# Two reversed chunks: one stationary operand with the keys of two chunks per recurrence level, and another order at the end of the recurrence

## What is computed

```python
f = lb + (1.0 - lb) * jax.nn.sigmoid(f_pre)
log_f, k, q, v = jnp.log(f), 1.0 - f, jax.nn.silu(q_pre), i_in
def step(state, inp):
    qc, kc, vc, lfc = inp
    b = jnp.cumsum(lfc, axis=2)
    o_inter = jnp.einsum('bhtd,bhde->bhte', qc * jnp.exp(b), state)
    decay = jnp.where(causal, jnp.exp(b[t] - b[s]), 0.0)          # [t, s, d]
    a = jnp.einsum('bhtd,bhsd,bhtsd->bhts', qc, kc, decay)
    o_intra = jnp.einsum('bhts,bhse->bhte', a, vc)
    b_last = b[:, :, -1:, :]
    state = jnp.exp(b_last) * state + jnp.einsum('bhsd,bhse->bhde', kc * jnp.exp(b_last - b), vc)
    return state, o_inter + o_intra
o = o * lax.rsqrt(jnp.mean(o * o, axis=-1, keepdims=True) + NORM_EPS)
o = o.reshape(B, S, E) * out_norm * jax.nn.silu(g_pre)
return o @ w_out
```

## Time and profile before

| | |
|---|---|
| median of 3 runs | 2952.06 us (2950.47 to 2953.12) |
| profiled execution, its own time | 2953.08 us |
| its span | 2951.2 us |
| PE busy | 2922.4 us, 99% of the span |
| DVE, POOL, ACT busy | 80%, 44%, 40% |
| granted TensorE clock | 0.999 of 2.4 GHz |
| the recurrence | from 1555.7 to 1684 us of the span |

### The profile page before, as it was taken

How to read it: one execution, slowest core, us unless ns; L and a number is a source line. 1 busy time by engine, 2 the same in 40 slices (tenths; PEclk the granted TensorE clock), 3 DMA queues, 4 the chain that set the end, 5 groups by cost and what they waited for, 6 DMA issues and landing times.

```text
span 2951.2 us, 43795 instructions
## 1 busy us (share of the span) xinstructions
PE 2922.4 (99%) x16066; PEld 2617.8 (89%) x16066; DVE 2363.7 (80%) x4421; ACT 1192.1 (40%) x1853; POOL 1296.6 (44%) x747
## 2 busy tenths in 40 slices
PE   8999999999999999999999999999999999999999
PEld 7778999999998888888889988999999998888887
DVE  7538999989878888888356747999888878888887
ACT  6543334444433333333435533333444433333333
POOL 4133565334444444442447443654444444444441
PEclk9999999999999999999999999999999999999999
DMA  4032558999999999998321032659999999999995
GB/s 156 31 106 86 172 177 319 372 357 355 379 377 398 362 361 359 363 361 293 100 93 44 30 107 79 196 179 366 363 360 374 359 399 387 363 362 361 359 365 212
DMA packets 346148, 799.76 MB, mean 271 GB/s; under 512 B 27984, under 2 KB 192080, under 8 KB 345680
## 3 DMA queue, kind: packets, MB, share of 16 engines
q1 hardware_dynamic: 235200, 478.09, 46.3%
q0 software_dynamic: 73728, 268.47, 23.8%
q10 hardware_dynamic: 37008, 50.41, 4.6%
HBM read 694.10 MB, written 102.76 MB: 270 GB/s over the span
## 4 chain that ended last, share of the span: by engine, by line
PE 97%; DVE 1%; ACT 1%; issue 0%; DMA 0%; POOL 0%; DVEq 0%; SPq 0%
PE PS L1644 29%; PE PS L1646 29%; PE PS L1645 29%; PE PS L1865 3%; PE PS L1946 2%; PE PS L1844 1%; PE PS L1774 1%; PE PS L1775 1%; PE PS L1821 1%; DVE resid L1089 1%; ACT arena L690 0%; PE PS L1809 0%; PE PS L1654 0%; PE PS L1655 0%; PE PS L1949 0%
## 5 line engine op out<-in xcount | busy, mean ns | idle before, releaser
L677 ACT ACTIVATE w_hi<-w_raw 128x1024 fp32r<-128x1024 f32 x607 | 641.8, 1059 | 816.5 <-PE PS L1646 678.7
L1644 PE MATMUL PS<-x_hi,w_hi 128*128 128x384 f32 (+1 forms) x2564 | 897.2, 350 | 0.0
L1646 PE MATMUL PS<-x_hi,w_lo 128*128 128x384 f32 (+1 forms) x2564 | 886.4, 346 | 0.0
L1645 PE MATMUL PS<-x_lo,w_hi 128*128 128x384 f32 (+1 forms) x2564 | 884.9, 345 | 0.0
L1644 PE MATMUL PS<-w_hi,x_hi 128*128 128x512 f32 x1744 | 679.6, 390 | 0.8 <-ACT arena L771 0.8
L1646 PE MATMUL PS<-w_hi,x_lo 128*128 128x512 f32 x1744 | 678.6, 389 | 0.0
L1645 PE MATMUL PS<-w_lo,x_hi 128*128 128x512 f32 x1744 | 678.5, 389 | 0.0
L614 POOL DMA_INDIRECT arena<-in_v_t,arena x256 | 427.7, 1671 | 553.0 <-DVE resid L1387 525.1
L603 POOL TENSOR_TENSOR w_lo<-w_raw,w_hi 128x1024 fp32r<-128x1024 f32 x167 | 414.3, 2486 | 513.6 <-ACT w_hi L677 513.6
L1364 DVE TENSOR_TENSOR w_lo<-w_raw,w_hi 128x1024 fp32r<-128x1024 f32 x440 | 536.7, 1220 | 108.0 <-ACT w_hi L677 105.1
L614 POOL DMA_INDIRECT arena<-in_u_rows,arena x256 | 384.6, 1502 | 498.6 <-DVE arena L1371 444.3
(11 more groups left out here) (205 smaller groups left out, 2360.6 us busy)
## 6 DMA issues: line engine op xcount, KB each, us to landing
w_raw<-in_u_t SPq DMA_DIRECT2D x256, 512.0 KB
w_raw<-in_v_t SPq DMA_DIRECT2D x256, 512.0 KB
acts_dram<-arena ACTq DMA_DIRECT2D x256, 192.0 KB
gates_dram<-arena SPq DMA_DIRECT2D x24, 2048.0 KB
arena<-acts_dram SPq DMA_DIRECT2D x256, 192.0 KB
arena<-gates_dram SPq DMA_DIRECT2D x64, 768.0 KB
w_raw<-in_hg_t SPq DMA_DIRECT2D x40, 512.0 KB
w_raw<-in_pq_t SPq DMA_DIRECT2D x32, 512.0 KB
```

The source lines that it names most:

```text
L677: act.activation(w_hi[:, slot, :], w_raw[:, slot, :], ACT.Copy).then_inc(hi_ready, 1)
L1644: pe.matmul(ps, wh, xh, start=start, stop=False)
L1645: pe.matmul(ps, wh, xl, start=False, stop=False)
L1646: return pe.matmul(ps, wl, xh, start=False, stop=stop)
```

## The change

The tokens of chunks 2 and 3 are held in reverse (`TIME`), from the input on; the host puts the rows back at the end. In a reversed chunk the first half of a block's places holds the later tokens. So at each level the places of keys in chunks 0 and 1 are those of queries in chunks 2 and 3, and the other way round. The keys of chunk c and of chunk c + 2, 64 each, fill one stationary operand of 128 columns without gaps, and the moving operand holds the 64 queries of chunk c and the 64 of chunk c + 2. That is two matmuls of 128 x 128 for four of 128 x 64 at each of 56 levels. The masks drop the products between the two chunks.

What follows from it:

- `scale_level` is two instructions of 256 elements (keys, then queries) in place of one of 512.
- `take_diff` and the exponents read and write in patterns of two halves; their counts and element counts stay.
- `tensor_tensor_scan`, the cumulated sum, is two scans of 256 per head, the second one backward, in place of one of 512.
- The masks of the levels are 256 columns wide each; `mask_bits` grows from 1696 to 2592 columns of two bytes. `causal` gets a reversed twin for the attention in chunks 2 and 3.
- The gain of the output norm moves from DVE's `gate_head` (now a `tensor_tensor`) to ACT's copy in `head_out`.
- At the end of the recurrence spread 4 comes ahead of values and output of head 7, hss and the spreads 5 to 7 come earlier, and `project` of half rows 0 and 1 is split in two and laid between spreads. ACT's `gated_high(4)` comes ahead of `head_out(7)`, DVE's `gated_low(4)` and `gated(5)` ahead of `gate_head(7)`.

```diff
@@ -84,7 +84,10 @@
-M_LEVEL, M_IOTA, M_PAIR, M_COLS = SEQ, SEQ + 8 * P, SEQ + 9 * P, SEQ + 9 * P + 2 * TOPK
+M_SAME, M_LEVEL = SEQ, SEQ + P
+M_IOTA = M_LEVEL + LEVELS * SEQ // 2
+M_PAIR, M_COLS = M_IOTA + P, M_IOTA + P + 2 * TOPK
+TIME = [*range(SEQ // 2), *range(SEQ - P - 1, SEQ // 2 - 1, -1), *range(SEQ - 1, SEQ - P - 1, -1)]
@@ -218,19 +221,21 @@
                 yield "gate", part // KC, part % KC
                 part += 1
         if n >= 2 and (n - 2) % 8 == 7:
+            if n > 8 * HEADS:
+                yield "spread", 4, 0
             yield "values", (n - 2) // 8, 0
             yield "ho", (n - 2) // 8, 0
         if n % 8 == 0 and n >= 16:
             yield "hss", n // 8 - 2, 0
             if n == 8 * HEADS:
                 yield "project", 0, (2, 3)
-    yield "project", 0, (0, 1)
-    yield "spread", 4, 0
+    yield "spread", 5, 0
     yield "hss", HEADS - 1, 0
-    yield "spread", 5, 0
+    yield "project", 0, (0,)
     yield "spread", 6, 0
+    yield "project", 0, (1,)
+    yield "spread", 7, 0
     yield "project", 2, (0, 1, 2, 3)
-    yield "spread", 7, 0
 def plan():
...
@@ -408,11 +412,21 @@
-        def keys_and_queries(h, m):
-            both = arena[:, h * SEQ:h * SEQ + SEQ]
-            return bass.AP(both.tensor, both.offset,
-                           [list(both.ap[0]), [2 * m, SEQ // (2 * m)], [HEADS * SEQ + m, 2], [1, m]])
+        def of_halves(ap, first, second, step, count, inner, size):
+            return bass.AP(ap.tensor, ap.offset + first,
+                           [list(ap.ap[0]), [second - first, 2], [step, count], [inner, size]])
+        def level_keys(ap, m):
+            return of_halves(ap, 0, SEQ // 2 + m, 2 * m, P // m, 1, m)
+        def level_queries(ap, m):
+            return of_halves(ap, m, SEQ // 2, 2 * m, P // m, 1, m)
+        def backward(ap):
+            n = ap.shape[-1]
+            return bass.AP(ap.tensor, ap.offset + n - 1, [list(ap.ap[0]), [-1, n]])
@@ -632,16 +646,16 @@
+                half, b = SEQ // 2, gb[:, h, :]
-                    b4 = chunked(gb[:, h, :])
-                    ins = pool.tensor_tensor(chunked(d), b4[:, :, P - 1:P].broadcast_to([P, TT, P]), b4,
-                                             ALU.subtract)
+                    ins = pool.tensor_tensor(of_halves(d, 0, half, P, 2, 1, P),
+                                             of_halves(b, P - 1, half, P, 2, 0, P),
+                                             of_halves(b, 0, half, P, 2, 1, P), ALU.subtract)
-                    bb = gb[:, h, :].rearrange("p (b m) -> p b m", m=2 * m)
-                    ins = pool.tensor_tensor(d.rearrange("p (b m) -> p b m", m=2 * m), bb,
-                                             bb[:, :, m - 1:m].broadcast_to([P, SEQ // (2 * m), 2 * m]),
-                                             ALU.subtract)
+                    ins = pool.tensor_tensor(of_halves(d, 0, half, 2 * m, P // m, 1, 2 * m),
+                                             of_halves(b, 0, half, 2 * m, P // m, 1, 2 * m),
+                                             of_halves(b, m - 1, half + m, 2 * m, P // m, 0, 2 * m), ALU.subtract)
@@ -948,17 +962,16 @@
-                def halves(ap):
-                    return ap.rearrange("p (b s m) -> p b s m", s=2, m=P >> k)
-                act.activation(halves(scaling(n))[:, :, 0], halves(d)[:, :, 0], ACT.Exp, scale=-1.0)
-                act.activation(halves(scaling(n))[:, :, 1], halves(d)[:, :, 1], ACT.Exp)\
-                   .then_inc(sem("level_exp"), 1)
+                m = P >> k
+                by_part = scaling(n).rearrange("p (w s b m) -> p w s b m", w=2, s=2, m=m)
+                act.activation(by_part[:, 0], level_keys(d, m), ACT.Exp, scale=-1.0)
+                act.activation(by_part[:, 1], level_queries(d, m), ACT.Exp).then_inc(sem("level_exp"), 1)
-                free(act.activation(gq[:, h, :], PSb(("ho", h)), ACT.Copy), ("ho", h))
+                g = G_AT["out"] + h
+                free(act.activation(gq[:, h, :], PSb(("ho", h)), ACT.Copy, scale=gain[:, g:g + 1]), ("ho", h))
@@ -1007,8 +1020,8 @@
             gated_high(3)
             roots(1)
             next_high(BASE["hg_g"] + HEADS - 1)
+            gated_high(4)
             head_out(HEADS - 1)
-            gated_high(4)
             roots(2)
             gated_high(5)
             gated_high(6)
...
@@ -1448,8 +1461,11 @@
-                dve.tensor_tensor_scan(gb[:, h, :], keep, diff[:, h % 2, :], 0.0, ALU.mult, ALU.add)\
-                   .then_inc(sem("cumulated"), 1)
+                early, late = slice(0, SEQ // 2), slice(SEQ // 2, SEQ)
+                dve.tensor_tensor_scan(gb[:, h, early], keep[:, early], diff[:, h % 2, early], 0.0,
+                                       ALU.mult, ALU.add)
+                dve.tensor_tensor_scan(backward(gb[:, h, late]), keep[:, early], backward(diff[:, h % 2, late]), 0.0,
+                                       ALU.mult, ALU.add).then_inc(sem("cumulated"), 1)
@@ -1464,10 +1480,12 @@
-                def halves(ap):
-                    return ap.rearrange("p (b s m) -> p b s m", s=2, m=P >> k)
-                dve.tensor_tensor(halves(xx[:, x % 2, :]), keys_and_queries(h, P >> k), halves(d), ALU.mult)\
+                m = P >> k
+                factor = d.rearrange("p (w s b m) -> p w s b m", w=2, s=2, m=m)
+                keys = xx[:, x % 2, 0:SEQ // 2].rearrange("p (b s m) -> p s b m", s=2, m=m)
+                queries = xx[:, x % 2, SEQ // 2:SEQ].rearrange("p (s b m) -> p s b m", s=2, m=m)
+                dve.tensor_tensor(keys, level_keys(gk[:, h, :], m), factor[:, 0], ALU.mult)
+                dve.tensor_tensor(queries, level_queries(gq[:, h, :], m), factor[:, 1], ALU.mult)\
@@ -1479,17 +1497,15 @@
-                                           level_mask[LEVELS].unsqueeze(1).broadcast_to([P, TT, P]), ALU.mult),
+                                           same_place.unsqueeze(1).broadcast_to([P, TT, P]), ALU.mult),
-                m, half = P >> p, P // 2
-                blocks = half // m
-                kept = a_sb[:, h % 2, :].rearrange("p (c b s m) -> p c b s m", c=TT, s=2, m=m)[:, :, :, 1]
-                given = PSb(("a", h, p))[:, 0:TT * half].rearrange("p (c b m) -> p c b m", c=TT, m=m)
-                where = mask_bits[:, M_LEVEL + P * (p - 1):M_LEVEL + P * (p - 1) + half]
-                where = where.rearrange("p (b m) -> p b m", m=m).unsqueeze(1).broadcast_to([P, TT, blocks, m])
-                free(dve.copy_predicated(kept, where, given), ("a", h, p))
+                m, n = P >> p, SEQ // 2
+                given = PSb(("a", h, p))[:, 0:n].rearrange("p (s b m) -> p s b m", s=2, m=m)
+                where = mask_bits[:, M_LEVEL + n * (p - 1):M_LEVEL + n * p]
+                free(dve.copy_predicated(level_queries(a_sb[:, h % 2, :], m),
+                                         where.rearrange("p (s b m) -> p s b m", s=2, m=m), given), ("a", h, p))
...
@@ -1508,9 +1524,7 @@
-                g = G_AT["out"] + h
-                dve.scalar_tensor_tensor(gq[:, h, :], gq[:, h, :], gain[:, g:g + 1], gg_[:, h, :],
-                                         ALU.mult, ALU.mult).then_inc(sem("head_gain"), 1)
+                dve.tensor_tensor(gq[:, h, :], gq[:, h, :], gg_[:, h, :], ALU.mult).then_inc(sem("head_gain"), 1)
@@ -1575,10 +1589,10 @@
             head_rstd(1)
             gated(4)
             gate_silu(7)
+            gated_low(4)
+            gated(5)
             gate_head(7)
             head_mean(7)
-            gated(5)
-            gated_low(4)
             head_rstd(2)
             gated(6)
             gated_low(5)
...
@@ -1939,12 +1949,12 @@
-                    for c in range(TT):
-                        t = slice(c * P, (c + 1) * P)
+                    for c in range(TT // 2 if p else TT):
+                        t, part = slice(c * P, (c + 1) * P), slice(c * P // 2, (c + 1) * P // 2)
-                            both = xx[:, x % 2, t]
-                            mm = pe.matmul(PSb(("a", h, p))[:, c * P // 2:(c + 1) * P // 2], both,
-                                           upper(both, p), start=True, stop=True)
+                            queries = xx[:, x % 2, SEQ // 2:SEQ].rearrange("p (s n) -> p s n", s=2)[:, :, part]
+                            given = PSb(("a", h, p))[:, 0:SEQ // 2].rearrange("p (s n) -> p s n", s=2)[:, :, part]
+                            mm = pe.matmul(given, xx[:, x % 2, t], queries, start=True, stop=True)
@@ -2024,20 +2034,21 @@
-    c[:, C_IOTA:C_IOTA + P] = np.arange(P)
-    c[:, C_CAUSAL:C_CAUSAL + P] = np.where(np.arange(P)[None, :] <= np.arange(P)[:, None], 0.0, -1e30)
+    s, t = np.arange(P)[:, None], np.arange(P)[None, :]
+    c[:, C_CAUSAL:C_CAUSAL + 2 * P] = np.concatenate([np.where(t <= s, 0.0, -1e30), np.where(t >= s, 0.0, -1e30)], 1)
-    s, t = np.arange(P)[:, None], np.arange(P)[None, :]
-        keep = (s // (2 * half) == t // (2 * half)) & (s // half % 2 == 0)
```

(12 more changed lines are left out.)

13 lines of the change are left out of this document (5 added, 8 removed).

## The result

The changed kernel takes 2933.36 us (median of 4 runs, 2932.46 to 2934.11), the kernel before 2951.26 (4 runs, 2949.86 to 2953.12): a ratio of 0.9943, 95% interval 0.993 to 0.9957. The profiled execution took 2932.46 us, its span is 2930.3.

What follows compares the result with a forecast made beforehand. PE was taken as the bound, with DVE 4 us per head behind; 17.0 us from the recurrence plus 1.2 from its end made 18.2 off 2953.1, and 1.0 for the median gave 2934.0 (2933.9), range 2930 to 2944.

Steps and rivals of the forecast that it cites:

- PE's levels: Recurrence's level matmuls on PE: halved records take a level from 0.84 to 0.445 us, 22.1 over 56 levels.
- DVE's scalings: Scaling at each level: two multiplies of 256 cost 0.08 to 0.28 us more than one of 512; 0.08 taken.
- Heads 2 to 4: Steady heads: PE stays the bound, a(4) 0.1 us late, each head 13.5 us, 2.7 less.
- Heads 0 and 1: First heads: 2.2 us gained with early levels paced by DVE's masks, then 2.0 with 0.8 staying with POOL.
- Head 5: Counted as a steady head, with the same gain of 2.7 us.
- Heads 6 and 7: 0.8 us gained until a(2) of head 6, then 1.2 to the last level, limited by DVE's little idle time.
- The end: Behind the last level: the new order removes PE's wait before spread 6, 1.2 us.
- Edits at nothing: Scans, larger mask load, moved gain and reversed attention chunks: costed at nothing.
- 1: Rival: DVE becomes the bound, a pair of multiplies costing 0.88 us; gain 8.3 to 9, about 2943.5 us; chance 0.24.
- 2: Rival: all of PE's gain arrives, 23.3 us, giving 2928.7; chance 0.05.
- 3: Rival: the level matmul gets no cheaper, staying at 0.84 us, leaving 1.2 us of gain, 2951; chance 0.06.
- 4: Rival: POOL's differences double to 2.1 us, some 20 us slower in all, 2971; chance 0.03.

Runs made afterwards that it cites:

- later groups: The unedited kernel before, run again beside each group of follow-up kernels: medians 2948.98, 2948.89 and 2948.67 us.
- second comparison: Changed kernel and kernel before run once more, with no edit: 2934.91 against 2948.89 us, ratio 0.9946.
- kernel with its levels twice: Changed kernel with each of the 56 x 2 level matmuls issued twice in a row: 2947.96 us, recurrence 125.9.
- cut into four: Changed kernel with each scaling in four multiplies of 128 elements in place of two of 256: 2938.49 us, recurrence 113.8.
- early copy: Changed kernel with ACT's copy of the transposed decayed keys one step earlier: 2932.37 us, recurrence 109.3.
- moved square root: Changed kernel with early copy, head 7's three low halves moved to POOL, and first square root moved from head 5 to 6: 2931.84 us, recurrence 109.1.

## Why the prediction was right, and by which steps

The time was right (2934.0 against 2933.36), and partly by luck, since two errors of some 3 us cancel. 18.2 us were forecast and the change is worth 14.7; and the sum starts from a median of before, 2952.06, that lay 3 us above the 2948.7 to 2949.0 of the later groups (its profiled execution carried 5.0 us of chance waits). From 2948.9 the same sum would have given 2931, against 2934.91 in the second comparison.

- **PE's levels.** The mechanism was right, 224 records and 0.44 to 0.46 us a level. The term of 0.395 us per level was 0.05 too small, 2.8 us over the 56 levels: the levels before cost 0.89, by the kernel with its levels twice.
- **DVE's scalings.** 0.08 more per pair was forecast, 0.06 measured; the upper bound of 0.28 had no ground, by the cut into four. The section of the Trainium skill that the prediction holds against the pair (VectorE: DVE Perf Modes, "The DRAIN you can't avoid") goes on: "A next op that is not held starts earlier". So the starts 0.60 apart at a duration of 0.68 do not contradict it, as the prediction has it.
- **Heads 2 to 4.** 2.7 forecast, 2.5 measured: 3.1 of work less 0.6 of waiting for the mask of step 2. The place was right, and so was the time at which a(4) starts on the chain (7.34 us after a(0) forecast, 1597.67 - 1590.38 = 7.29 measured). The size was not ("0.1 us late"): from start to start the delay is 0.3, and the restart, which I left out, another 0.3.
- **Heads 0 and 1.** 2.2 and 2.0 forecast, 1.66 and 1.52 measured. The early copy gives back 0.44 and 0.54 us: ACT's copy, which I had costed at nothing, was late next, and POOL was not the only one.
- **Head 5.** 2.7 forecast, 1.28 measured, the largest miss. I gave head 5 the gain of a steady head and never asked what ACT does there: two table loads and a late copy. The early copy gives 0.48 back and the moved square root 0.7, most of the miss. Before, PE's 17.10 us covered them.
- **Heads 6 and 7.** 2.0 forecast, 2.8 measured, with DVE at 13.36 of 14.01 us in head 7. DVE is the bound there as I had it, but had more idle time to fill than the 2.1 us I counted (my row of head 7 ends 1.1 us before the last level does). The two heads before:

```profile
1649.71:1665.61 15.90, 15.90 (x129) 15.24 (x128) 11.95 (x25) 9.09 (x22) 11.31 (x10) 1.00 0.11 35
1665.61:1681.18 15.57, 15.37 (x122) 14.39 (x121) 13.74 (x27) 7.88 (x20) 5.13 (x5) 1.00 0.01 2
```

  DVE's idle time in them fell from 5.8 to 2.1 us, and its busy time rose by 0.8.
- **The end.** 1.2 forecast, 0.0 measured. The new order takes its wait away, and more than I said (1.5), but with the idle stretches of PE ahead of it, which the shorter levels make, comes a granted clock of 0.50 that costs 1.5 us. The sum has no term for the clock.
- **Edits at nothing.** Nothing in the traces contradicts them: the rest of the span is no longer than before, and with the levels twice the recurrence is 125.9 us against 125.7. The scans and masks were not tried alone.

Of the rivals, 1 is refuted as priced and right in its direction in head 7; 2 failed because DVE or ACT makes PE wait in every head; 3 and 4 did not occur (the differences take 1.17 us in the mean, 1.14 before).

## What to carry to other kernels

When the bound engine's work is cut, ask of every head, the odd ones too, which rare instruction the old work covered (a table load, a copy): it is late next. Price a wait on TensorE as the wait and a restart (0.3 us here), and look whether the granted clock is lower in what follows. Read the cost of a matmul from start to start with the row behind it, and where the rest of the program wanders by a good part of the gain, read the gain from the trace's own stretch.

## What was not expected of the hardware

- Matmuls of 64 columns pay their full 0.11 us per record, as those of 128 do, but 0.05 us of each level's end shows up in the next instruction's row.
- A restart of PE after a wait costs 0.31 us beside the wait (head 3; heads 2 to 4 lose 0.6 us each to both, which fits).
- The granted clock fell to 0.50 for 3.4 us behind the levels of the changed kernel, and stayed at 1.00 in the kernel whose PE had idled 0.33 us less in the 8 us ahead; with the early copy it stayed at 1.38 us of idle time against 1.45. So little idle time went with 1.5 us. What exactly sets it stays open.
- A table load takes 1.28 us, and the activation starts 0.02 us behind it. The Trainium skill (ScalarE: Activation LUTs, "What ACT_TABLE_LOAD costs") adds a drain of 1380 ns to each switch; no such gap stands ahead of or behind the loads here.
- One DVE instruction more over the same elements costs 0.06 to 0.07 us from start to start.
